# Two transformer stacks on one core: start order, load times, item shapes and split work rearranged

## What is computed

```python
def first_block(x, c, ...):
    for layer, mixer in enumerate((nsa_mixer, dilated_mixer)):
        h, gate = adaln_norm(x, c, norm_g[layer], ada_w[layer], ada_b[layer])
        x = x + gate * mixer(h, ...)
    return rms_norm(x, final_g)

def second_block(x, ...):
    for layer, mixer in enumerate((_mixer_ab, _mixer_cd)):
        x = _layer_norm(x + mixer(x, ...), ln1_g[layer], ln1_b[layer])
        x = _layer_norm(x + _swiglu(x, w_gate[layer], w_up[layer], w_down[layer]), ...)
    return x
```

## Time and profile before

| | us |
|---|---|
| median of 3 runs | 1076.28 |
| runs | 1076.28, 3453.79, 1075.4 |
| profiled execution | 1067.2 |
| its span, first to last instruction | 1065.4 |
| mean granted TensorE clock | 0.987 of full speed |

### The profile page before, as it was taken

How to read it: one execution, slowest core, us unless ns; L and a number is a source line. 1 busy time by engine, 2 the same in 40 slices (tenths; PEclk the granted TensorE clock), 3 DMA queues, 4 the chain that set the end, 5 groups by cost and what they waited for, 6 DMA issues and landing times.

```text
span 1065.4 us, 15899 instructions
## 1 busy us (share of the span) xinstructions
PE 995.3 (93%) x6092; PEld 843.8 (79%) x6092; DVE 658.4 (62%) x1154; ACT 460.9 (43%) x702; POOL 127.9 (12%) x114
## 2 busy tenths in 40 slices
PE   5999988889999999989989999999998999999995
PEld 2899755779997678977778888887997778888884
DVE  4456454774663676655856666667446586666666
ACT  1343444624454633555334444433436434444441
POOL 3005101210970001020100000000003000000000
PEclk9999999999999999999999999999999999999998
DMA  9963254334453355420465554443633144555441
GB/s 377 363 221 135 94 223 159 125 152 158 160 206 103 144 190 190 163 80 9 161 227 185 202 203 179 177 154 112 221 127 120 63 177 160 195 206 186 177 177 39
DMA packets 23669, 178.40 MB, mean 167 GB/s; under 512 B 3743, under 2 KB 4175, under 8 KB 7111
## 3 DMA queue, kind: packets, MB, share of 16 engines
q1 hardware_dynamic: 19408, 166.70, 42.6%
q0 software_dynamic: 2224, 8.94, 2.6%
q10 hardware_dynamic: 1991, 2.14, 0.6%
HBM read 176.72 MB, written 1.05 MB: 167 GB/s over the span
## 4 chain that ended last, share of the span: by engine, by line
PE 78%; DVE 11%; DMA 4%; ACT 3%; issue 2%; ACTq 1%; POOL 0%; SPq 0%; DVEq 0%; POOLq 0%
PE G L951 13%; PE G L952 13%; PE G L953 13%; PE S L1057 7%; PE T L1057 7%; PE S L1056 3%; PE T L1056 3%; PE T L586 3%; PE T L481 2%; PE G L602 1%; DMA ring<-in_ada_w 1%; PE G L601 1%; PE G L600 1%; PE G L405 1%; DVE wlo L1767 1%
## 5 line engine op out<-in xcount | busy, mean ns | idle before, releaser
L951 PE MATMUL G<-whi,hTh 128*128 128x256 f32 (+4 forms) x688 | 221.7, 322 | 9.5 <-DVE hTl L522 7.3
L1892 DVE TENSOR_TENSOR wlo<-ring,whi 128x2048 fp32r<-128x2048 f32 x88 | 154.4, 1759 | 95.4 <-ACT whi L1548 63.2
L952 PE MATMUL G<-wlo,hTh 128*128 128x256 f32 (+4 forms) x672 | 210.7, 313 | 0.0
L953 PE MATMUL G<-whi,hTl 128*128 128x256 f32 (+4 forms) x624 | 191.4, 307 | 0.0
L951 PEld LDWEIGHTS G<-whi,hTh 128*128 128x128 f32 x688 | 132.1, 192 | 17.7 <-DVE hTl L522 8.6
L1764 DVE TENSOR_TENSOR wlo<-ring,whi 128x1024 fp32r<-128x1024 f32 (+2 forms) x60 | 92.6, 1585 | 67.4 <-ACT whi L1443 67.2
L1057 PE MATMUL S<-hT,whi 128*128 128x512 f32 x352 | 129.3, 401 | 3.7 <-DVE wlo L1892 3.7
L952 PEld LDWEIGHTS G<-wlo,hTh 128*128 128x128 f32 x672 | 128.9, 192 | 3.9 <-issue 1.5
L1057 PE MATMUL T<-hT,whi 128*128 128x512 f32 x352 | 126.4, 394 | 0.0
L953 PEld LDWEIGHTS G<-whi,hTl 128*128 128x128 f32 x624 | 119.7, 192 | 0.7
L1543 ACT CAST whi<-ring 128x2048 fp32r<-128x2048 f32 x44 | 83.8, 1905 | 24.4 <-PE S L1128 17.6
(11 more groups left out here) (331 smaller groups left out, 1821.0 us busy)
## 6 DMA issues: line engine op xcount, KB each, us to landing
ring<-in_ffn SPq DMA_DIRECT2D x44, 1536.0 KB, 6.4
ring<-in_ada_w SPq DMA_DIRECT2D x16, 1024.0 KB, 6.3
ring<-in_dil_w_in SPq DMA_DIRECT2D x16, 1024.0 KB, 4.8
ring<-in_cd_w_in SPq DMA_DIRECT2D x10, 1232.0 KB, 5.4
ring<-in_nsa_w_in SPq DMA_DIRECT2D x8, 1432.0 KB, 8.5
early<-in_ada_w SPq DMA_DIRECT2D x8, 1024.0 KB, 17.2
ring<-in_ab_w_in SPq DMA_DIRECT2D x4, 1440.0 KB, 6.2
vec<-in_vecs POOLq DMA_DIRECT2D x11, 512.0 KB, 5.2
```

The source lines that it names most:

```text
L951: pe.matmul(out_, act_h, w_h, start=first_, stop=False)
L952: pe.matmul(out_, act_h, w_l, start=False, stop=False)
L953: return pe.matmul(out_, act_l, w_h, start=False, stop=last_)
L1892: TT(wlo[b][:, part], ring[:, b, part], whi[b][:, part].bitcast(F32), ALU.subtract).then_inc(st[what + "_lo"], 1)
```

## The change

- `EARLY` becomes (2, 0, 3, 1): scale and shift of the first 512 channels come first, then those of the second. Between the blocks TensorE does the first half of the contraction of nsa_in's item 0 (`first_products`, 24 matmuls), and nsa_in is in `HALVED`.
- ScalarE issues only the tables and pe_rows ahead of nsa_in's first eviction; the other loads stand behind the casts of items 2 and 3.
- dil_in has 16 items of 512 columns and half the contraction, written out for TensorE (`dil_item`, `dil_block`). The turn of tile 1 follows after 12 matmuls.
- dil_out joins `APART`, and GpSimd splits items 0 and 1 in all three stages. The casts on ScalarE and subtractions on VectorE of these items are gone, `low_quarters` too.
- The shares of the first 14 heads are worked out ahead, the last ones before the last pair is gated (`take_shared`).
- At borders `between` is called for one half before `turn_low` and for the other behind it. Before an FFN it makes the gate half only; the up half follows the turn of tile 1.
- GpSimd waits for `act_ready` of the fourth FFN step before vectors 5 and 6, with the three bias loads behind them, and in ffn1 before 9 and 10.

```diff
-EARLY = (2, 3, 0, 1)
+EARLY = (2, 0, 3, 1)
-DIL_C, DIL_W = 16, 256
+DIL_C, DIL_W, DIL_K = 8, 512, KT // 2
-HALVED = ("dil_in", "ab_in", "cd_in")
+HALVED = ("nsa_in", "dil_in", "ab_in", "cd_in")
-        APART = ("ab_out", "cd_out")
+        APART = ("dil_out", "ab_out", "cd_out")
...
             def split_item(name):
-                n = first[name] + 1
-                pool.wait_ge(landed[n % 2], 16 * (n // 2 + 1))
                 pool.wait_ge(used, split0[name] - 1)
+                for item in range(2):
+                    n = first[name] + item
+                    pool.wait_ge(landed[n % 2], 16 * (n // 2 + 1))
...
             load_vec(3)
+            pool.wait_ge(woven["turned"], woven0["dil"] + 4)
+            split_item("dil_out")
...
             rstd_of(5)
+            pool.wait_ge(ffn[0]["act_ready"], 4)
             load_vec(5)
...
+            def first_products(t, half):
+                pe.wait_ge(turn["low"], turns["h0"][3] + 2 * half + t + 1)
+                if t == 0:
+                    pe.wait_ge(lo_done, part0["nsa_in"] + half + 1)
...
-                keep_busy(2, S[(b + 1) % 2], ident)
+                if b == 2:
+                    first_products(0, 0)
+                else:
+                    keep_busy(2, S[(b + 1) % 2], ident)
...
-            gemm("dil_in", proj["dil_in"], DIL_C, DIL_W, 0, "h1", norm_tiles(1), 4)
+            def dil_item(m, j, t, block):
+                wh, wl = (part[j][:, 0:DIL_K * DIL_W].rearrange("p (k w) -> p k w", k=DIL_K) for part in (whi, wlo))
+                for k in range(DIL_K):
+                    if t == 0 and k % 2 == 0:
+                        pe.wait_ge(lo_done, m * 2 + (part0["dil_in"] + 1 + k // 2))
+                    kk, ts = j * DIL_K + k, slice(t * P, (t + 1) * P)
+                    ins = split_products(G[2 * block + t][:], ...)
+                return ins
+            dil_item(0, 0, 0, 0)
+            turn_pe(pe, "h1", norm_tiles(1), 1)
+            dil_item(1, 1, 0, 0).then_inc(st["full"], 1)
...
-            high_out("ab_out", 0)
             turn_act(sc_e, "ab_rot")
...
                 evict(2, 1, 0)
-                between()
+                between(0)
                 turn_low(dve, turn_name, 0)
+                between(1)
                 evict(3, 1, 1)
...
+                if p == H // 2 - 1:
+                    shares(summed)
+                    share_group(0)
+                    share_group(1)
+                set_gated(p, o, summed, r, dil_s["gated"] if p == H // 2 - 1 else None)
...
-            low_out("ab_out", 0)
             turn_draw(dve, "ab_rot")
```

More of the change, by code:

```diff
@@ L1760, in low @@
                 if name in HALVED:
-                    for half in range(2):
+                    for half in halves:
                         at = slice(half * cols // 2, (half + 1) * cols // 2)
@@ L2176, in dil_steps @@
                 elif p == 8:
-                    low_quarters("dil_out", 0, (0, 1))
-            dve.wait_ge(proj["dil_in"]["taken"], 2 * DIL_C)
-            attention("dil", lambda i: table(f"dil{group[i]}"), set_gated, between=group_weights,
-                      behind=dil_steps)
-            dve.wait_ge(late["taken"], LATE)
-            dve.wait_ge(dil_s["lse_out"], 1)
-            done(dve.reciprocal(den[:], rden[:, 0:H, :]))
-            done(TT(lse[:, 0, :].rearrange("p (h t) -> p h t", t=NT), lse[:, 0, :].rearrange("p (h t) -> p h t", t=NT), den[:], ALU.mult))
@@ new lines, in shares @@
+            def shares(summed):
+                last = by_pair[:, H - 2:H, :]
+                done(TT(last.unsqueeze(3), last.unsqueeze(3), summed, ALU.mult))
+                done(dve.tensor_reduce(share[:, :, 2], by_head[:, :, offs[2]:offs[3]], AX.X, ALU.add))
+                done(TT(share, share, per_head, ALU.mult))
+                done(dve.tensor_reduce(top, share, AX.X, ALU.add))
+                done(dve.reciprocal(top, top))
+                done(STT(share, share, 3.0, over(top, 2, 3), ALU.mult, ALU.mult), dil_s["share"])
@@ L2197, in _ @@
+            dve.wait_ge(proj["dil_in"]["taken"], 2 * DIL_C)
+            attention("dil", lambda i: table(f"dil{group[i]}"), take_shared, between=group_weights,
+                      behind=dil_steps)
+            share_group(2)
+            dve.wait_ge(late["taken"], LATE)
             g_final = next_vec()
@@ L2205, in norm_2 @@
                 done(STT(x[:, t, :], x[:, t, :], rstd[:, t:t + 1], g_final, ALU.mult, ALU.mult), norm["ready"])
[L2207 removed]
+            project_out(1, "dil_out", mod1[:, 2 * D:3 * D], lambda half: low("ab_in", 0, 0, KT * AB_W, (half,)), norm_2, "x0", early=False, low_first=1)
             note(mod1_used)
@@ L2266, in _ @@
             g6, b6 = next_vec(), next_vec()
-            ffn_out(0, "ffn0", 6, g6, b6, "x1", lambda j: low("cd_in", 0, j, KT * CD_W))
+            ffn_out(0, "ffn0", 6, g6, b6, "x1", lambda j, halves: low("cd_in", 0, j, KT * CD_W, halves))
             note(vec_used)
```

250 lines of the change are left out of this document (156 added, 94 removed).

## The result

The changed kernel takes 1059.05 us in the median of four runs (1052.84 to 1064.81). Its ratio to the kernel before is 0.9866, with a 95% interval from 0.9824 to 0.9907: it is faster by about 14 us, clear of no change (a ratio of 1), and by less than 2%. The forecast was 1054, the range 1045 to 1067. The profiled execution took 1058.84 us, 8.4 us less than that of the kernel before.

The account below looks back on a forecast made before the run. TensorE was taken to bound the kernel, busy 995.3 of 1065.4 us. Gains of 24.4 us less 2.2 for the clock gave 22, from the median 1076.28 to 1054 us, range 1045 to 1067.

Parts of the forecast that it names:

- start to nsa_in's end (halves, loads): Program start: early matmuls of nsa_in gain 2.8 us; postponed loads and halved low parts gain 1.9 us.
- dil_in in 512 columns: dil_in: 512-column matmuls at 0.2275 us replace 256-column ones at 0.119 us, with the second turn fixed by VectorE; gain 2.9 us.
- end of dilated attention: Attention ends 1.1 us earlier, turn to low part gains another 1.1, item 2's earlier cast 0.8; sum 3.0 us.
- turn of ab: Before ab's first scores: copies of qT start earlier, waits of 1.87 and 0.83 us and 1.2 slow clock go; gain 3.9 us.
- ffn0: FFN 0: postponing three bias loads removes a 3.7 us wait and 1.7 us of low clock; gain 5.4 us.
- turn of cd: Before cd's first scores: the qT wait of 2.23 us goes, and 0.8 as in ab; gain 3.0 us.
- clock, unplaced: Three longer TensorE holes, at dil_in, ab_in and cd_in, bring 1.3 more clock drops than before; loss 2.2 us.
- clock falls at all three new holes: Rival: low clock follows each longer hole, at dil_in, ab_in and cd_in; gain 19.3 us, 1057 us; chance 0.25.
- The rival that GpSimd's second item would slow the attention: Three attention stages: GpSimd's splits slow VectorE, costing 20 to 28 us, 1080 us; chance 0.04.
- the fillers, which stay, are what the turn waits for, not the shares: End of dilated attention: TensorE's fillers, not VectorE's share sums, set the turn of the tokens; another 1.1 us gained.
- the rival that the stall only moves: ffn0: postponed bias loads still delay the ring's weight item, so TensorE stands as before; gain 16.6 us, 1060 us; chance 0.18.
- the two terms of 0.5: Before ffn0 and before ffn1: the shorter gate half frees VectorE for the eviction earlier; 0.5 us each, 1.0 together.

## Why the prediction was right, and where it was not

The time lies in the range. The gain, 14 us against 22 forecast, is short by a third. The range was wide, gains of 9 to 31 us, and that the medians of 1054 and 1059 lie close is in part luck: the forecast starts from a median of 1076.28, and the later medians of the same kernel are 1071.73 to 1073.56. In the profiled execution, where the terms were summed, 1045 was forecast and 1058.84 came.

The table goes through the two profiled executions by the stages of TensorE, in us gained (from first product to first product; where a stage's length holds slow clock it is named); its lines sum to the 8.4 us between the spans. The last column is an estimate of what the drops added to a stage or took from it, where TensorE bounded.

| stage | forecast | measured | part of slow clock |
|---|---|---|---|
| start to nsa_in's end (halves, loads) | 4.7 | 4.2 | |
| nsa attention | 0 | -6.7 | 5.8 more than before; 0.8 a longer wait for weights |
| dil_in in 512 columns | 2.9 | 0.5 | 3.1 more than before |
| end of dilated attention | 2.2 | -0.7 | |
| dil_out, its border | 1.25 | 0.6 | 0.8 more |
| turn of ab | 3.9 | 3.7 | 1.3 less |
| ab attention, ab_out | 0.5 | 1.6 | 1.6 less |
| ffn0 | 5.4 | 3.9 | 1.7 less |
| cd_in | 0.1 | 0 | |
| turn of cd | 3.0 | 2.9 | |
| cd attention, cd_out | 0.5 | -1.6 | 1.6 more |
| clock, unplaced | -2.2 | | |

The forecast's -2.2 for the clock stands against 6.7 us net in the last column. By the ledger alone it is 5.1 (10.2 lost up to the last matmul before, 15.4 after); the column has more mainly because the drop at 235 to 239 in the kernel before cost nothing, ahead of a turn that VectorE fixed. Without clock the edits sum to some 15 us against 21.5 (24.4 less the 1.2 and 1.7 of slow clock in the terms of ab and ffn0).

The clock explains why this pair of traces shows 8.4 us and not 14. It does not explain why 14 came and not 22. The kernel before has 24 executions beside the experiments, with a mean granted clock of 0.980, some 21 us lost in each; its profiled one had 0.987 and lost 13.9. The changed kernel's eight executions have a mean of 0.980 too. So over many executions the clock took the same from both, though the hole at dil_in brings its drop every time; where the kernel before loses as much, three traces of its order do not show. What fell short are the edits: most of all the end of dilated attention (2.9 us less than forecast), then ffn0 (1.5), the places ahead of the FFNs (1.0), the longer wait in the nsa attention (0.8) and the start (0.5); dil_in gave 0.7 more than forecast.

**Start**: the sum came (4.2 of 4.7), the split did not. The early products are worth 1.0 to 2.4 us and not 2.8, the other edits the rest; putting the loads back cost 5.6.

**Turns of ab and cd**: right in mechanism and, without clock, in size: 2.4 and 2.9 us against 2.7 and 3.0. The further 1.2 in the term of ab was slow clock of the one execution read. The rival that GpSimd's second item would slow the attention there is refuted by the run with one item.

**dil_in**: right in mechanism, the interval of 512 columns held, and the hole of some 6 us came where it was placed (5.7). (768 x 0.119 is 91.4 and not 91.7, which changes nothing.) But I priced the drop at 1.7 us, and gave three places an expected 1.3 of them. Here it was 3.3 to 3.4, every time. This is the rival "clock falls at all three new holes" at one place, twice as dear. The similar holes at ab_in and cd_in did not come: TensorE idles 1.8 us in ab_in, and 0.8 and 1.4 in cd_in, where the 1.4 had been before. A drop followed in two of the eight traces with the hole at ab_in unfilled, and at cd_in in four of eleven.

**End of dilated attention** failed, the step with "the fillers, which stay, are what the turn waits for, not the shares" and the 1.1 us for it. Neither trace has low clock there. TensorE's turn of the tokens behind its eight fillers, before and after:

```profile
370.76 3.65 PE L978 MATMUL G<-tab 128*128 128x512 f32 x8
375.27 1.09 PE L481 MATMUL S<-tab,tok 128*128 128x128 f32 x8 [0.86 <-ACT tok L1682]
...
372.09 3.65 PE L981 MATMUL G<-tab 128*128 128x512 f32 x8
377.32 1.09 PE L483 MATMUL S<-tab,tok 128*128 128x128 f32 x8 [1.57 <-ACT tok L1775]
```

From dil_in's last product to these fillers it takes 38.1 us, 0.7 less than before (1.1 forecast). From the fillers to dil_out's first product it takes 8.1 us, 1.4 more than before (1.1 less forecast): the turn waits longer, and the first product waits 0.9 us for the low part. On VectorE, operations with two operands in SBUF were held by GpSimd's, of which the share product stood 1.4 us longer on the path to the turn. The Trainium skill, in "SBUF — State Buffer", section "Who interferes with whom", has this rule, an exclusive lock on a shared pair of ports; the trace agrees, with two operations that end within 0.03 us of each other (375.57 and 375.54). I had it as a rival for the score reductions, which read PSUM and did stay at 0.42, and did not ask which other operations stand beside the split. That this is the whole of the missing 2.5 us is not shown.

**ffn0**: right in mechanism, and the size was that of a full cure. ScalarE waited 4.07 us for step 5's item, 0.63 with the loads apart: the three together made it some 3.4 us late, where I had counted 3 of slack, and TensorE stood 1.14 us. So the rival that the stall only moves held for a fourth of the term, 1.4 of 5.4 us; that part came when the loads were set apart.

**Ahead of the FFNs**: the two terms of 0.5 came to nothing. From ab_out's first product to ffn0's first it takes 32.1 us in the changed kernel, and 32.1 in the kernel before with spaced loads, where no drop falls in it. VectorE's second eviction begins 0.4 us earlier. It can't begin sooner, since it waits 0.6 us for the projection's last products, and TensorE's eight fillers stand ahead of the next turn as before.

**Clock**: the profiled execution of the kernel before, against which I summed, had none of the 5.1 us that its second trace shows in the nsa attention. The correction of 2.2 would have covered most of dil_in's drop alone. Over a whole execution the changed kernel, its repetition and the one with spaced loads lost 18.9, 22.2 and 23.9 us, the kernel before 13.9 in the trace that I summed against and 19.0 in the other.

## What to carry to other kernels

Read the granted clock in fine windows before summing small gains, and in more than one execution: the trace of the kernel before had lost 7 us less than its executions did on average. Here a stage made faster with a longer hole ahead paid most of its gain back in slow clock, and fillers in the hole kept the clock up and did not delay the turn. Where the bank is in use, a filler with zero weights can stand in it. Where work moves to GpSimd, list VectorE's operations beside it by where their operands lie: here those with two in SBUF were held (1.59 us for 0.17), those that read PSUM were not (0.42).

## What had not been expected of the hardware

The length of a slow stretch did not follow that of the hole ahead of it: in the nsa attention holes of 1.3 to 2.0 us were followed by losses of up to 5.1 us, the hole of 5.7 at dil_in by 3.3. What decides this is left open. In the dilated attention 3.4 to 6.8 us were lost in ten of fourteen traces. Three of the kernels are the same up to there (the changed one, its repetition and the one with spaced loads), and had none, none and 5.1: the same program, another execution. Such differences account for most of the spread of a kernel's executions: the changed kernel's fastest, 1052.84 us, had a mean clock of 0.984 (17 us lost), its slowest, 1064.81 us, one of 0.976 (26 us lost).
